# The forget gate's steps moved ahead of the first head pair's square, its memsets ahead of the mean square

## The chip, the cores and the metric

The kernel runs on one core of a Trainium2 chip. The metric is the device time of one execution in microseconds (us); what is quoted is the median of three runs. Everything is float32; to keep float32 accuracy on TensorE, most operands are split into a high and a low part, so that one product becomes three matmuls.

## The reference, cut to what matters

Two layers on a sequence of 1024 tokens with width 1024: first a short gated convolution, then an attention layer with a forget gate. The change touches the attention layer's start only.

```
h = rmsnorm(x, norm_g)
proj = h @ w_in                       # q | k | v | gate | forget, 4*1024 + 16 columns
q, k = rmsnorm(heads(q), q_g), rmsnorm(heads(k), k_g)     # per head of 64, 16 heads
log_f = log_sigmoid(proj[forget] + b_f)                   # 16 heads x 1024 tokens
c = cumsum(log_f, axis=tokens)
s = q @ k.T / 8 + c[query] - c[key]   # causal, then softmax, then @ v
x = x + (attention * silu(gate)) @ w_out
```

## The kernel before

All five engines have their instruction order written out by hand; they meet through counting semaphores (`s_f`, `s_fa` and so on), and each engine takes its instructions strictly in that order. Names used below: PE is TensorE, DVE VectorE, ACT ScalarE, POOL GpSimd, SP the engine that issues the loads and stores.

**Seam between the layers.** When the last convolution output has been added to `xy`, PE runs the 32 small matmuls of the forget columns (L686, into banks 4 and 5), then four of the mean square (L691). DVE meanwhile clears the stacks `q2`/`k2` with four memsets of 64 rows (`set_stacks(0.0, DH)`, L1604), adds EPS to the mean square (L1611), ACT makes a first guess of the reciprocal root as exp(-0.5 ln) (L1119, L1121), and DVE refines it to `inv`, the inverse norm of every token (L1614 to L1616). No projection can be evacuated before `inv` is there.

**Iteration 0 of the attention layer** projects the first head pair, and has no attention of its own. It has eight positions i = 0 to 7. At position i PE computes unit i, of 24 matmuls of 512 columns (L564): units 0 and 1 are the two halves of q, 2 and 3 of k, 4 and 5 of the gate, 6 and 7 of v. Units alternate between two banks, so unit i may start only when unit i - 2 has been evacuated by DVE (`qk_evac`, L1727; `vz_evac`, L1741). For each of the four q and k halves u the head norm follows, one position later each:

- ACT squares the half (`square`, L1295, at position u + 1), POOL makes the square's low part in two steps (`square_lo`, L1927, L1929),
- PE averages it over the head (`head_square`, L770 and L771), at position u + 2, between the fourth and the fifth eighth of that position's unit,
- ACT guesses the reciprocal root (`guess`, L1286, L1288), DVE refines it in four steps (`refine`, L1708 to L1714).

POOL's order is fixed too: `square_lo` of half 0 stands ahead of the low part of the weights for units 4 and 5 (`w_low`, L1907).

**The forget gate** is 16 rows of 1024 elements, and is worked out in iteration 0 in three parts, each of which DVE and ACT run at positions of their own. Part 0 on DVE (L1624 to L1633) adds the two halves of the logits, multiplies with `inv`, adds the bias, takes min(f, 0) and -|f|; part 0 on ACT is exp and ln(1 + .) (L1138, L1140). Part 1 on DVE fills `ones` with 1.0 (L1636), subtracts (L1638) and scans (L1640, the cumulative sum); on ACT it copies the high part of the sum (L1143). Part 2 is the low part (DVE, L1643) and the two negated copies (ACT, L1147, L1149). SP stores the four rows to `c_dram`, waits until all four have landed, and loads them into `q2` and `k2` (L469, L471). The first scores of iteration 1 (L714) wait for these rows. In DVE's position 1 stand four memsets of 4 rows that put 1.0 into `q2`/`k2` (`set_stacks(1.0, 4)`, L1604).

The positions of the parts are two short lists:

```
if not att and i in (2, 4, 5):        # DVE: parts 0, 1, 2
if not att and i in (3, 5, 6):        # ACT: parts 0, 1, 2
```

On ACT the part stands ahead of `square` of the same position. On DVE it stands behind the evacuation and `refine` of the same position. Iterations 1 to 8 run the attention of pair it - 1 beside the projection of pair it.

Of the kernel before, what the change touches and what calls it, by code (L numbers as in the profile page):

```python
# [7 lines left out]
ALU = mybir.AluOpType  # L8
ACT = mybir.ActivationFunctionType
# [5 lines left out]
KT = D // P  # L15
KH = KT // 2
NH = 16
# [90 lines left out]
def hybrid(nc, x, w_cin, w_cout, w_ain, w_forget, w_aout, conv_gain, conv_taps, attn_gain, b_forget,  # L108
# [5 lines left out]
    with ExitStack() as ctx:  # L114
        def sb(name, shape, dt=F32, where=ctx):
            return where.enter_context(nc.sbuf_tensor(name, shape, dt))

        def sem(name):
            return ctx.enter_context(nc.semaphore(name))
# [14 lines left out]
        b_f = sb("b_f", [NH, 1])  # L134
# [32 lines left out]
        y2 = sb("y2", [P, KT, S])  # L167
# [157 lines left out]
        def halves(h):  # L325
            return slice(h * HALF, (h + 1) * HALF)
# [49 lines left out]
        def _(sp):  # L376
# [77 lines left out]

            def store_c():

                sp.wait_ge(s_fa, 3)
                sp.dma_start(c_dram[:, 0, :], pt_hi[0:NH, :, :].bitcast(F32)).then_inc(s_cst, 16)
                sp.wait_ge(s_f, 8)
                sp.dma_start(c_dram[:, 1, :], pt_lo[0:NH, :, :].bitcast(F32)).then_inc(s_cst, 16)  # L460
                sp.wait_ge(s_fa, 4)
                sp.dma_start(c_dram[:, 2, :], v_st[0:NH, 0, :, :].bitcast(F32)).then_inc(s_cst, 16)
                sp.wait_ge(s_fa, 5)
                sp.dma_start(c_dram[:, 3, :], v_st[0:NH, 1, :, :].bitcast(F32)).then_inc(s_cst, 16)

            def c_rows(side, pair):
# [448 lines left out]
        def _(act):  # L915
            A = nc.scalar.activation
# [210 lines left out]
            def forget_low():  # L1127

                act.wait_ge(s_unit, 2 * N_FORGET + 2)
                for h in range(2):  # L1130
                    ins = A(p_big[0:NH, 1, halves(h)], ps[2 * NH:3 * NH, 4 + h, :], ACT.Copy)
                ins.then_inc(s_fc, 1)

            def forget(part):
                f = p_big[0:NH, 0, :]
                if part == 0:
                    act.wait_ge(s_f, 5)
                    A(f, f, ACT.Exp).then_inc(s_fa, 1)  # L1138
                    act.wait_ge(s_fa, 1)
                    A(f, f, ACT.Ln, bias=1.0).then_inc(s_fa, 1)  # L1140
                if part == 1:
                    act.wait_ge(s_f, 7)
                    A(pt_hi[0:NH, :, :], f.rearrange("p (a n) -> p a n", a=2), ACT.Copy).then_inc(s_fa, 1)  # L1143
                if part == 2:
                    act.wait_ge(s_fa, 3)
                    act.wait_ge(s_f, 8)
                    A(v_st[0:NH, 0, :, :], pt_hi[0:NH, :, :].bitcast(F32).rearrange("p a n -> p (a n)"),  # L1147
                      ACT.Copy, scale=-1.0).then_inc(s_fa, 1)
                    A(v_st[0:NH, 1, :, :], pt_lo[0:NH, :, :].bitcast(F32).rearrange("p a n -> p (a n)"),  # L1149
                      ACT.Copy, scale=-1.0).then_inc(s_fa, 1)  # L1150
# [70 lines left out]
            def iteration(it, proj, att, before):  # L1221
                for i in range(8):
# [29 lines left out]
                        guess(it, i - 2)  # L1252
                    if not att and i == 0:
                        forget_low()
                    if not att and i in (3, 5, 6):
                        forget((3, 5, 6).index(i))
                    if proj and i == (6 if att else 5):
                        stack_q_hi(it, 0)
                    if chunks > 2:
# [61 lines left out]
            with act.Fori(2, PAIRS) as it:  # L1321
                iteration(it, True, True, True)
# [11 lines left out]
        def _(dve):  # L1334
            v = nc.vector
            TT, TS, STT = v.tensor_tensor, v.tensor_scalar, v.scalar_tensor_tensor
# [262 lines left out]
            def set_stacks(value, rows):  # L1599

                for side in range(2):
                    r = DH * (1 - side)
                    for st in (q2, k2):
                        ins = v.memset(st[r:r + rows, side, :].bitcast(F32), value)  # L1604
                ins.then_inc(s_clear, 1)

            dve.wait_ge(s_co, 2 * KT)
            set_stacks(0.0, DH)
            for h in range(2):
                dve.wait_ge(s_ms, h + 1)  # L1610
                TS(mbuf[:, h, :], ps[:, 6 + h, :], EPS, None, ALU.add).then_inc(s_msr, 1)  # L1611
# [6 lines left out]
            def forget(part):  # L1618

                f, m0, ones = p_big[0:NH, 0, :], p_big[0:NH, 1, :], y2[0:NH, KT - 1, :]  # L1620
                if part == 0:
                    dve.wait_ge(s_fc, 1)
                    for h in range(2):
                        ins = TT(f[:, halves(h)], ps[0:NH, 4 + h, :], m0[:, halves(h)], ALU.add)  # L1624
                    ins.then_inc(s_f, 1)
                    dve.wait_ge(s_f, 1)
                    TT(f, f, inv[0:NH, :], ALU.mult).then_inc(s_f, 1)
                    dve.wait_ge(s_f, 2)
                    TS(f, f, b_f[:, :], None, ALU.add).then_inc(s_f, 1)
                    dve.wait_ge(s_f, 3)  # L1630
                    TS(m0, f, 0.0, None, ALU.min).then_inc(s_f, 1)
                    dve.wait_ge(s_f, 4)
                    STT(f, m0, 2.0, f, ALU.mult, ALU.subtract).then_inc(s_f, 1)  # L1633
                if part == 1:
                    dve.wait_ge(s_spill, 16 * KT)
                    v.memset(ones, 1.0)  # L1636
                    dve.wait_ge(s_fa, 2)
                    TT(m0, m0, f, ALU.subtract).then_inc(s_f, 1)  # L1638
                    dve.wait_ge(s_f, 6)
                    v.tensor_tensor_scan(f, ones, m0, 0.0, ALU.mult, ALU.add).then_inc(s_f, 1)  # L1640
                if part == 2:
                    dve.wait_ge(s_fa, 3)
                    TT(pt_lo[0:NH, :, :].rearrange("p a n -> p (a n)"), f,  # L1643
                       pt_hi[0:NH, :, :].bitcast(F32).rearrange("p a n -> p (a n)"), ALU.subtract)\
                        .then_inc(s_f, 1)
# [97 lines left out]
            def iteration(it, proj, att, before, base):  # L1743
                local = 0
                for i in range(8):
# [30 lines left out]
                        v_low(it - 1, 1)  # L1776
                    for c in range(2, chunks):
                        pt_low(own, at, c)
                    if not att and i == 1:
                        dve.wait_ge(s_clear, 1)  # L1780
                        set_stacks(1.0, 4)
                    if att:
                        invert(it, i, 1)
                    if proj and 2 <= i <= 5:
                        local = refine(it, i - 2, base, local)
                    if not att and i in (2, 4, 5):
                        forget((2, 4, 5).index(i))
                    if proj and i == 7:
                        stack_q_lo(it, 0)
                    if not proj and i == 0:  # L1790
# [235 lines left out]
```

## Time and profile before

| | |
|---|---|
| median of 3 runs | 1173.52 us (1173.18 to 1174.07) |
| the profiled execution | 1173.42 us, of which its span 1171.6 us |
| PE busy | 1130.5 us, 96% of the span |
| DVE, ACT, POOL busy | 775.2, 578.8, 608.1 us |
| iteration 0 on PE | about 438.4 to 491.45 us |
| mean granted TensorE clock | 0.991 |

The span runs from the first to the last instruction; the time of the execution is 1.8 us longer. A row of the timeline gives start, duration, engine, line, what is written and read, and in brackets how long the engine had been idle and who released it. Matmuls overlap, so a row of 0.39 us starts 0.23 us after the one before. In a row of the windows stand: the stretch, its length, busy time (and count) of PE, PE's weight loads, DVE, ACT and POOL, the granted TensorE clock (1.00 is 2.4 GHz), the DMA share and GB/s.

### The profile page before, as it was taken

To read this page: it belongs to the slowest core of one execution; us is meant where nothing else is said; L and a number is where in the kernel's file an instruction comes from. 1 tells how busy PE (TensorE), PEld (TensorE's weight loads), DVE (VectorE), ACT (ScalarE), POOL (GpSimd) and SP (SyncE) were. 2 spreads that over 40 slices of the span, in tenths; PEclk is the share of its full clock that TensorE was granted. 3 is DMA by queue.
4 is the path that set the end of the run, shared out by engine and by line. 5 is a ranking of instruction groups with operands and counts; after the bars stand their busy time and mean duration, and the time that the engine had idled before them with its cause. 6 is when DMAs were issued, how large, how long until landed. Compare 5 with 4: busy or idle time off the path is not lost.

```text
span 1171.6 us, 16915 instructions
## 1 busy us (share of the span) xinstructions
PE 1130.5 (96%) x5652; PEld 920.8 (79%) x5652; DVE 775.2 (66%) x1056; ACT 578.8 (49%) x982; POOL 608.1 (52%) x400
## 2 busy tenths in 40 slices
PE   5999999999999998999999999999999999978998
PEld 3688888888888876787887878878878788767887
DVE  3997778566865238668667586686675866875541
ACT  5553232333334324665755757657557575575410
POOL 2235665555546434556475664664755646655410
PEclk8999999999999999999999999999999999989999
DMA  6201102110144211200110101001101010002142
GB/s 216 73 1 72 70 4 72 72 72 19 54 162 151 92 58 63 58 26 19 38 37 1 42 31 37 18 18 36 36 2 52 19 36 18 18 18 89 56 160 75
DMA packets 20256, 64.17 MB, mean 55 GB/s; under 512 B 2928, under 2 KB 3056, under 8 KB 20208
## 3 DMA queue, kind: packets, MB, share of 16 engines
q1 hardware_dynamic: 20064, 63.53, 16.0%
q8 instruction: 29, 0.48, 0.2%
q14 instruction: 19, 0.16, 0.0%
q10 hardware_dynamic: 144, 0.00, 0.0%
HBM read 54.88 MB, written 8.65 MB: 54 GB/s over the span
## 4 chain that ended last, share of the span: by engine, by line
PE 85%; DVE 8%; issue 3%; ACT 2%; DMA 1%; POOL 1%; ACTq 0%; DVEq 0%; SPq 0%
PE ps L564 33%; PE ps L581 26%; PE ps L754 6%; PE ps L662 6%; PE ps L714 5%; PE ps L735 5%; DVE neg_max L1657 1%; DVE newton L1712 1%; PE ps L575 1%; PE ps L777 1%; PE ps L718 1%; PE ps L686 1%; DMA raw<-in_w_cout 1%; DVE b_lo L1502 1%; DVE newton L1708 1%
## 5 line engine op out<-in xcount | busy, mean ns | idle before, releaser
L564 PE MATMUL ps<-h_hi,w_hi 128*128 128x512 f32 x632 | 267.6, 423 | 5.8 <-DVE h_lo L1803 2.5
L564 PE MATMUL ps<-h_hi,w_lo 128*128 128x512 f32 x632 | 249.2, 394 | 0.0
L564 PE MATMUL ps<-h_lo,w_hi 128*128 128x512 f32 x632 | 248.4, 393 | 0.0
L1868 POOL TENSOR_TENSOR a_lo<-raw,a_hi 128x512 fp32r<-128x512 f32 x94 | 136.5, 1463 | 160.9 <-ACT a_hi L955 160.9
L581 PE MATMUL ps<-b_hi,a_hi 128*128 128x512 f32 x456 | 180.0, 395 | 8.0 <-DVE b_lo L1375 7.9
L581 PE MATMUL ps<-b_lo,a_hi 128*128 128x512 f32 x456 | 178.4, 391 | 0.0
L581 PE MATMUL ps<-b_hi,a_lo 128*128 128x512 f32 x456 | 178.3, 391 | 0.0
L564 PEld LDWEIGHTS ps<-h_hi,w_lo 128*128 128x128 f32 x632 | 119.1, 189 | 27.2
L1907 POOL TENSOR_TENSOR w_lo<-w_raw,w_hi 128x1024 fp32r<-128x1024 f32 x39 | 99.1, 2542 | 78.3 <-ACT w_hi L923 78.1
L1916 POOL TENSOR_TENSOR p_big<-p_big,rdenom 128x896 f32<-128x896 f32 (+1 forms) x64 | 93.8, 1466 | 87.8 <-DVE rdenom L1665 87.7
L1657 DVE TENSOR_REDUCE neg_max<-ps 128x1 f32<-128x896 f32 (+7 forms) x128 | 96.4, 753 | 62.3 <-PE ps L718 61.8
L564 PEld LDWEIGHTS ps<-h_hi,w_hi 128*128 128x128 f32 x632 | 120.2, 190 | 22.2 <-issue 3.6
L1671 DVE TENSOR_TENSOR pt_lo<-ps,pt_hi 128x512 fp32r<-128x512 f32 (+1 forms) x160 | 97.2, 633 | 53.4 <-ACT pt_hi L1180 51.1
L564 PEld LDWEIGHTS ps<-h_lo,w_hi 128*128 128x128 f32 x632 | 120.3, 190 | 15.0 <-issue 0.2
L1916 POOL TENSOR_TENSOR p_small<-p_small,rdenom 128x640 f32<-128x640 f32 (+1 forms) x64 | 70.6, 1104 | 115.6 <-DVE rdenom L1665 114.4
L955 ACT ACTIVATE a_hi<-raw 128x512 fp32r<-128x512 f32 x94 | 58.0, 628 | 121.5 <-PE ps L581 43.9
L581 PEld LDWEIGHTS ps<-b_hi,a_hi 128*128 128x128 f32 x456 | 86.1, 189 | 29.4 <-DVE b_lo L1375 10.3
L581 PEld LDWEIGHTS ps<-b_hi,a_lo 128*128 128x128 f32 x456 | 86.2, 189 | 18.2
L581 PEld LDWEIGHTS ps<-b_lo,a_hi 128*128 128x128 f32 x456 | 86.2, 189 | 17.9 <-issue 0.5
L1180 ACT ACTIVATE pt_hi<-ps 128x512 fp32r<-128x512 f32 (+1 forms) x160 | 83.1, 551 | 33.3 <-PE ps L735 31.9
L714 PE MATMUL ps<-k,q 128*128 128x512 f32 (+5 forms) x384 | 92.8, 351 | 5.8 <-ACT p_big L1170 3.6
L714 PEld LDWEIGHTS ps<-k,q 128*128 128x128 f32 x384 | 69.6, 191 | 23.4 <-ACT p_big L1170 7.0
(182 smaller groups left out, 2109.9 us busy)
## 6 DMA issues: line engine op xcount, KB each, us to landing
w_raw<-in_w_ain SPq DMA_DIRECT2D x32, 512.0 KB, 3.3
raw<-in_w_cin SPq DMA_DIRECT2D x28, 512.0 KB, 4.2
xy<-in_x SPq DMA_DIRECT2D x16, 512.0 KB, 4.7
raw<-in_w_cout SPq DMA_DIRECT2D x8, 512.0 KB, 4.4
x_dram<-xy SPq DMA_DIRECT2D x8, 512.0 KB, 4.2
w_raw<-in_w_aout SPq DMA_DIRECT2D x8, 512.0 KB, 4.3
out<-y SPq DMA_DIRECT2D x7, 512.0 KB, 7.1
raw<-in_w_cin SPq DMA_DIRECT2D x8, 256.0 KB, 8.6
```

Of the source, the lines that this page charges most:

```text
L564: last = mm(ps[:, bank, :], st[slot][:, k, :], mov(k)[:, halves(h)], start=(at == 0 and (when or k == 0) and st is w_hi and mov is mov_hi) ...
L581: ins = mm(ps[:, bank, :], st[:, i % RING, k, :], mov[:, k, :], start=(first and st is a_hi and mov is b_hi[b]), stop=(last and st is a_lo ...
L662: ins = mm(ps[:, BANKS[u % 8], :], st[:, i, k % KH, :], mov[Y_SLOT + s][:, 2 * c + h, :], start=(first and k == ks[0] and st is a_hi and m ...
L714: last = mm(ps[:, bank, 0:w], a[:, side, qs:qs + P], b[:, side, c * w:(c + 1) * w], start=(a is q1), stop=(a is q2 and not last_c))
L735: last = nc.tensor.transpose(ps[:, B_PT + g % 2, at:at + P], src[:, par, (2 * c + kp) * P:(2 * c + kp + 1) * P], ident[:, :])
L754: last = mm(ps[:, B_OUT, at + skip:at + 2 * P], v_st[:, side, 2 * c + kp, :], mov[:, g % 2, kp * 2 * P:(kp + 1) * 2 * P - skip], start=(c ...
L1180: A(pt_hi[:, g % 2, 0:w], ps[:, B_PT + g % 2, 0:w], ACT.Copy).then_inc(s_pth, 1)
L1657: v.tensor_reduce(neg_max[:, col:col + 1], src, ax, ALU.max, negate=True).then_inc(s_max, 1)
L1671: TT(pt_lo[:, g % 2, 0:w], ps[:, B_PT + g % 2, 0:w], pt_hi[:, g % 2, 0:w].bitcast(F32), ALU.subtract).then_inc(s_ptl, 1)
L1868: TT(a_lo[:, i % RING, :, :], entry_source(i), a_hi[:, i % RING, :, :].bitcast(F32), ALU.subtract).then_inc(s_alo, 1)
L1907: TT(w_lo[slot][:, :, :], w_raw[:, slot, :, :], w_hi[slot][:, :, :].bitcast(F32), ALU.subtract).then_inc(s_wlo, 1)
L1916: TT(p, p, rdenom[:, col:col + 1].broadcast_to([P, w]), ALU.mult).then_inc(s_pn, 1)
```

## The change

On DVE, the four memsets of 1.0 and the memset of `ones` move from positions 1 and 4 to a place behind the four of 0.0, ahead of the reading of the mean square. Part 0 of the forget gate moves from position 2 to 1 on DVE, parts 1 and 2 from 4 and 5 to 5 and 6. On ACT the parts move from 3, 5, 6 to 1, 6, 7. The bias addition and the minimum become one DVE instruction; the separate bias addition and the step to -|f| go, and ACT takes |f + b| itself, and gives exp a scale of -1. SP's waits are renumbered.

```
             def forget(part):                                        # ACT
                 f = p_big[0:NH, 0, :]
                 if part == 0:
-                    act.wait_ge(s_f, 5)
-                    A(f, f, ACT.Exp).then_inc(s_fa, 1)
+                    act.wait_ge(s_f, 3)
+                    A(f, f, ACT.Abs, bias=b_f[:, :]).then_inc(s_fa, 1)
                     act.wait_ge(s_fa, 1)
+                    A(f, f, ACT.Exp, scale=-1.0).then_inc(s_fa, 1)
+                    act.wait_ge(s_fa, 2)
                     A(f, f, ACT.Ln, bias=1.0).then_inc(s_fa, 1)
...
-                    if not att and i in (3, 5, 6):
-                        forget((3, 5, 6).index(i))
+                    if not att and i in (1, 6, 7):
+                        forget((1, 6, 7).index(i))
...
             dve.wait_ge(s_co, 2 * KT)
             set_stacks(0.0, DH)
+            dve.wait_ge(s_clear, 1)
+            set_stacks(1.0, 4)
+            v.memset(y2[0:NH, KT - 1, :], 1.0)
             for h in range(2):
                 dve.wait_ge(s_ms, h + 1)
                 TS(mbuf[:, h, :], ps[:, 6 + h, :], EPS, None, ALU.add).then_inc(s_msr, 1)
...
                     TT(f, f, inv[0:NH, :], ALU.mult).then_inc(s_f, 1)
                     dve.wait_ge(s_f, 2)
-                    TS(f, f, b_f[:, :], None, ALU.add).then_inc(s_f, 1)
-                    dve.wait_ge(s_f, 3)
-                    TS(m0, f, 0.0, None, ALU.min).then_inc(s_f, 1)
+                    TS(m0, f, b_f[:, :], 0.0, ALU.add, ALU.min).then_inc(s_f, 1)
+                if part == 1:
+                    dve.wait_ge(s_fa, 3)
+                    TT(m0, m0, f, ALU.subtract).then_inc(s_f, 1)
                     dve.wait_ge(s_f, 4)
-                    STT(f, m0, 2.0, f, ALU.mult, ALU.subtract).then_inc(s_f, 1)
-                if part == 1:
-                    dve.wait_ge(s_spill, 16 * KT)
-                    v.memset(ones, 1.0)
-                    dve.wait_ge(s_fa, 2)
-                    TT(m0, m0, f, ALU.subtract).then_inc(s_f, 1)
-                    dve.wait_ge(s_f, 6)
                     v.tensor_tensor_scan(f, ones, m0, 0.0, ALU.mult, ALU.add).then_inc(s_f, 1)
...
-                    if not att and i == 1:
-                        dve.wait_ge(s_clear, 1)
-                        set_stacks(1.0, 4)
...
-                    if not att and i in (2, 4, 5):
-                        forget((2, 4, 5).index(i))
+                    if not att and i in (1, 5, 6):
+                        forget((1, 5, 6).index(i))
```

DVE's instructions from the last memset of 0.0 to the first `refine`, before the change:

```order
L1604 MEMSET k2 64x1024
L1611 TENSOR_SCALAR sq2<-ps 128x512 [waits mean_square_done] x2
L1614 TENSOR_TENSOR acc<-inv 128x1024 [waits rsqrt_guessed]
L1615 SCALAR_TENSOR_TENSOR acc<-acc,sq2 128x1024 [waits vector_steps]
L1616 SCALAR_TENSOR_TENSOR inv<-acc,inv 128x1024 [waits vector_steps]
L1727 TENSOR_TENSOR qn<-ps,inv 128x512 [waits units_done,x1_stored,vector_steps]
L1604 MEMSET q2 4x1024 [waits stacks_cleared]
L1604 MEMSET k2 4x1024
...
L1727 TENSOR_TENSOR qn<-ps,inv 128x512 [waits units_done]
L1708 TENSOR_TENSOR newton<-y0 128x512 [waits head_rsqrt_guessed]
```

And after it (lines past the added ones are shifted by a few; L1726 is the evacuation, L1707 the first step of `refine`):

```order
L1606 MEMSET k2 64x1024
L1606 MEMSET q2 4x1024 [waits stacks_cleared]
L1606 MEMSET k2 4x1024
...
L1613 MEMSET y2 16x1024
L1616 TENSOR_SCALAR sq2<-ps 128x512 [waits mean_square_done] x2
L1619 TENSOR_TENSOR acc<-inv 128x1024 [waits rsqrt_guessed]
...
L1726 TENSOR_TENSOR qn<-ps,inv 128x512 [waits units_done,x1_stored,vector_steps]
L1629 TENSOR_TENSOR p_big<-ps,p_big 16x512 [waits forget_lo_part_copied]
...
L1632 TENSOR_TENSOR p_big<-p_big,inv 16x1024 [waits forget_steps]
L1634 TENSOR_SCALAR p_big<-p_big,b_f 16x1024 [waits forget_steps]
L1726 TENSOR_TENSOR qn<-ps,inv 128x512 [waits units_done]
L1707 TENSOR_TENSOR newton<-y0 128x512 [waits head_rsqrt_guessed]
```

Five memsets have come in front of the reading of the mean square, and four steps of the forget gate between the evacuations of units 0 and 1.

ACT's instructions from the guess for `inv` to the first head's guess, before:

```order
L1121 ACTIVATE inv<-inv 128x1024 [waits rsqrt_guessed]
L923 ACTIVATE w_hi0<-w_raw 128x1024 [waits units_done,w_landed0]
L1131 ACTIVATE p_big<-ps 16x512 [waits units_done]
...
L1295 ACTIVATE sq_hi<-qn 128x512 [waits qk_evacuated]
L923 ACTIVATE w_hi1<-w_raw 128x1024 [waits units_done,w_landed1]
L1286 ACTIVATE y0<-ps,eps_col 128x512 [waits head_square_done]
```

And after:

```order
L1121 ACTIVATE inv<-inv 128x1024 [waits rsqrt_guessed]
L923 ACTIVATE w_hi0<-w_raw 128x1024 [waits units_done,w_landed0]
L1131 ACTIVATE p_big<-ps 16x512 [waits units_done]
...
L1138 ACTIVATE p_big<-p_big,b_f 16x1024 [waits forget_steps]
L1140 ACTIVATE p_big<-p_big 16x1024 [waits forget_act_steps]
L1142 ACTIVATE p_big<-p_big 16x1024 [waits forget_act_steps]
L1297 ACTIVATE sq_hi<-qn 128x512 [waits qk_evacuated]
L923 ACTIVATE w_hi1<-w_raw 128x1024 [waits units_done,w_landed1]
L1288 ACTIVATE y0<-ps,eps_col 128x512 [waits head_square_done]
```

The three ACT steps of part 0 now stand in front of the square of the first q half; PE's and SP's orders are unchanged.

## Rows read from the trace of the kernel before

**Rows 1.** The page: busy time by engine, and the chain by engine.

```profile
PE 1130.5 (96%) x5652; PEld 920.8 (79%) x5652; DVE 775.2 (66%) x1056; ACT 578.8 (49%) x982; POOL 608.1 (52%) x400
...
PE 85%; DVE 8%; issue 3%; ACT 2%; DMA 1%; POOL 1%; ACTq 0%; DVEq 0%; SPq 0%
```

**Rows 2.** Timeline of PE in iteration 0: unit 2, head squares, waits, first scores.

```profile
449.70 0.39 PE L564 MATMUL ps<-h_hi,w_hi 128*128 128x512 f32 x1
...
452.42 0.39 PE L770 MATMUL ps<-sq_hi,mean_h 128*128 128x512 f32 x1
...
464.25 0.47 PE L564 MATMUL ps<-h_hi,w_hi 128*128 128x512 f32 x1 [2.42 <-DVE kn L1727]
...
469.32 0.47 PE L770 MATMUL ps<-sq_hi,mean_h 128*128 128x512 f32 x1 [2.09 <-POOL sq_lo L1929]
...
491.45 0.97 PE L714 MATMUL ps<-k,q 128*128 128x448 f32 x4
```

**Rows 3.** Windows: two stretches of iteration 0.

```profile
461.67:469.32 7.65, 3.14 (x13) 2.21 (x13) 5.73 (x8) 3.59 (x4) 2.97 (x3) 1.00 0.00 0
...
470.50:474.00 3.50, 3.50 (x10) 2.68 (x10) 2.46 (x4) 1.40 (x3) 2.94 (x3) 0.51 0.39 132
```

**Rows 4.** Timeline of DVE from the last memset of 0.0 to evacuation 1.

```profile
436.73 0.91 DVE L1604 MEMSET k<- 64x1024 f32 x1 [0.16 <-issue]
...
438.97 0.69 DVE L1611 TENSOR_SCALAR sq<-ps 128x512 f32<-128x512 f32 x1 [0.17 <-PE ps L691]
...
443.20 3.30 DVE L1615 SCALAR_TENSOR_TENSOR acc<-acc,sq 128x1024 f32<-128x1024 f32 x1
446.53 1.23 DVE L1616 SCALAR_TENSOR_TENSOR inv<-acc,inv 128x1024 f32<-128x1024 f32 x1
447.79 0.69 DVE L1727 TENSOR_TENSOR qn<-ps,inv 128x512 f32<-128x512 f32 x1
448.75 0.91 DVE L1604 MEMSET q<- 4x1024 f32 x1 [0.27 <-issue]
...
452.90 0.62 DVE L1727 TENSOR_TENSOR qn<-ps,inv 128x512 f32<-128x512 f32 x1
```

**Rows 5.** Timeline of DVE: the forget gate's parts 0 and 1.

```profile
458.24 1.27 DVE L1624 TENSOR_TENSOR p_big<-ps,p_big 16x512 f32<-16x512 f32 x2
459.54 1.21 DVE L1627 TENSOR_TENSOR p_big<-p_big,inv 16x1024 f32<-16x1024 f32 x1
460.79 0.74 DVE L1629 TENSOR_SCALAR p_big<-p_big,b_f 16x1024 f32<-16x1024 f32 x1
...
463.43 0.67 DVE L1727 TENSOR_TENSOR kn<-ps,inv 128x512 f32<-128x512 f32 x1
...
475.43 0.91 DVE L1636 MEMSET y<- 16x1024 f32 x1 [0.15 <-issue]
476.27 1.15 DVE L1638 TENSOR_TENSOR p_big<-p_big 16x1024 f32<-16x1024 f32 x1
477.46 2.28 DVE L1640 TENSOR_TENSOR_SCAN p_big<-y,p_big 16x1024 f32<-16x1024 f32 x1
```

**Rows 6.** Timeline of ACT: squares, part 0, the last copy.

```profile
448.52 0.63 ACT L1295 ACTIVATE sq_hi<-qn 128x512 fp32r<-128x512 f32 x1 [4.58 <-DVE qn L1727]
...
463.53 1.06 ACT L1138 ACTIVATE p_big<-p_big 16x1024 f32<-16x1024 f32 x1 [3.04 <-DVE p_big L1633]
...
465.58 0.61 ACT L1295 ACTIVATE sq_hi<-kn 128x512 fp32r<-128x512 f32 x1
...
485.34 1.04 ACT L1149 ACTIVATE v_st<-pt_lo 16x1024 fp32r<-16x1024 f32 x1
```

**Rows 7.** Timeline of POOL: the first low part of weights.

```profile
442.93 2.49 POOL L1907 TENSOR_TENSOR w_lo<-w_raw,w_hi 128x1024 fp32r<-128x1024 f32 x1 [10.33 <-ACT w_hi L923]
```

**Rows 8.** One line's instructions: L1714 on k (duration min/median/max in ns).

```profile
L1714 DVE SCALAR_TENSOR_TENSOR kn<-kn,gk,newton x16: 752/1082/1655, 473.6 to 1019.2; 128x512 f32<-128x512 f32 x16
```

**Rows 9.** Timeline of SP: the first load of the stored rows into k2.

```profile
488.64 0.24 SPq L471 DMA_DIRECT2D k<-c_dram  x1
```

More of the change, by code:

```diff
@@ L455, in store_c @@
             def store_c():
-                sp.wait_ge(s_fa, 3)
+                sp.wait_ge(s_fa, 4)
                 sp.dma_start(c_dram[:, 0, :], pt_hi[0:NH, :, :].bitcast(F32)).then_inc(s_cst, 16)
-                sp.wait_ge(s_f, 8)
+                sp.wait_ge(s_f, 6)
                 sp.dma_start(c_dram[:, 1, :], pt_lo[0:NH, :, :].bitcast(F32)).then_inc(s_cst, 16)
-                sp.wait_ge(s_fa, 4)
+                sp.wait_ge(s_fa, 5)
                 sp.dma_start(c_dram[:, 2, :], v_st[0:NH, 0, :, :].bitcast(F32)).then_inc(s_cst, 16)
-                sp.wait_ge(s_fa, 5)
+                sp.wait_ge(s_fa, 6)
                 sp.dma_start(c_dram[:, 3, :], v_st[0:NH, 1, :, :].bitcast(F32)).then_inc(s_cst, 16)
@@ L1136, in forget @@
                 if part == 0:
-                    act.wait_ge(s_f, 5)
-                    A(f, f, ACT.Exp).then_inc(s_fa, 1)
+                    act.wait_ge(s_f, 3)
+                    A(f, f, ACT.Abs, bias=b_f[:, :]).then_inc(s_fa, 1)
                     act.wait_ge(s_fa, 1)
+                    A(f, f, ACT.Exp, scale=-1.0).then_inc(s_fa, 1)
+                    act.wait_ge(s_fa, 2)
                     A(f, f, ACT.Ln, bias=1.0).then_inc(s_fa, 1)
                 if part == 1:
-                    act.wait_ge(s_f, 7)
+                    act.wait_ge(s_f, 5)
                     A(pt_hi[0:NH, :, :], f.rearrange("p (a n) -> p a n", a=2), ACT.Copy).then_inc(s_fa, 1)
                 if part == 2:
-                    act.wait_ge(s_fa, 3)
-                    act.wait_ge(s_f, 8)
+                    act.wait_ge(s_fa, 4)
+                    act.wait_ge(s_f, 6)
                     A(v_st[0:NH, 0, :, :], pt_hi[0:NH, :, :].bitcast(F32).rearrange("p a n -> p (a n)"),
@@ L1628, in forget @@
                     dve.wait_ge(s_f, 2)
-                    TS(f, f, b_f[:, :], None, ALU.add).then_inc(s_f, 1)
-                    dve.wait_ge(s_f, 3)
-                    TS(m0, f, 0.0, None, ALU.min).then_inc(s_f, 1)
+                    TS(m0, f, b_f[:, :], 0.0, ALU.add, ALU.min).then_inc(s_f, 1)
+                if part == 1:
+                    dve.wait_ge(s_fa, 3)
+                    TT(m0, m0, f, ALU.subtract).then_inc(s_f, 1)
                     dve.wait_ge(s_f, 4)
-                    STT(f, m0, 2.0, f, ALU.mult, ALU.subtract).then_inc(s_f, 1)
-                if part == 1:
-                    dve.wait_ge(s_spill, 16 * KT)
-                    v.memset(ones, 1.0)
-                    dve.wait_ge(s_fa, 2)
-                    TT(m0, m0, f, ALU.subtract).then_inc(s_f, 1)
-                    dve.wait_ge(s_f, 6)
                     v.tensor_tensor_scan(f, ones, m0, 0.0, ALU.mult, ALU.add).then_inc(s_f, 1)
                 if part == 2:
-                    dve.wait_ge(s_fa, 3)
+                    dve.wait_ge(s_fa, 4)
                     TT(pt_lo[0:NH, :, :].rearrange("p a n -> p (a n)"), f,
```

## The prediction, made before the changed kernel ran

> **What bounds the kernel now.** I read the page first: PE is busy for 96% of the span and holds 85% of the chain that ended last [rows 1]. So a change elsewhere counts only where PE waits for it, and the question is which waits PE has in iteration 0, the one place the change touches. The timeline of PE there shows two: 2.42 us for the evacuation of unit 2, which stood behind DVE's part 0 of the forget gate, and 2.09 us for POOL's low square, whose input stood behind ACT's exp and ln [rows 2]. The window over both has PE busy for 3.14 of 7.65 us, so 4.5 us are lost. Behind them the clock is granted at 0.51, which is the 1.2 GHz level, for the 3.5 us from 470.5; before this PE ran at full clock and had just been idle for most of 7.65 us [rows 3]. Half clock for 3.5 us loses about 1.7 us. Together some 6.2 us are to be had here, and the change removes all of these causes. What is left to ask is what it puts in their place.
>
> The reader should see next how thin the margin is one step earlier. Unit 2 starts at 449.70, and its bank is free since evacuation 0, which ran from 447.79 for 0.69 us: 1.2 us of slack. The head square stands 12 matmuls later, at 452.42, and PE takes it without a wait, 3.90 us after ACT began the square at 448.52 [rows 2, 4, 6]. POOL's two steps between them fill most of these 3.9 us (the same stretch takes 465.58 to 469.32, 3.74 us, where PE does wait [rows 2, 6]), so this margin is only some 0.2 us, and everything in front of it hangs on `inv`.
>
> **The change, part by part.**
>
> *The memsets.* DVE ran the last memset of 0.0 at 436.73 and read the second half of the mean square at 438.97, with under half a microsecond idle between: there is no idle stretch in front of the reading, it lies behind it. Four memsets of 4 rows took from 448.75 to 452.90, 4.15 us, and that of `ones` 0.84 us (475.43 to 476.27) [rows 4, 5]. Four rows cost as much as 64 (0.91 us either way). The new second reading starts at 436.73 + 1.04 + 4.15 + 0.84 + 0.62 (the first reading, like an evacuation) = 443.4, or up to 443.8 with the gaps that memsets leave between them; I take 443.6, 4.6 us late. `inv` follows at fixed steps, so evacuation 0 starts at 447.79 + 4.6 = 452.4. From an evacuation's start to PE's restart it is 464.25 - 463.43 = 0.82 us [rows 2, 5]: unit 2 starts at 453.2 instead of 449.70, **a new wait of 3.5 us**.
>
> One step of this chain can change its length. L1615 took 3.30 us while L1616, of the same size, took 1.23; from 442.93 to 445.42 POOL ran its weight step beside it [rows 4, 7]. Both engines are released by the same ACT steps, so both shift by 4.6 and meet again: I keep 3.30. The Trainium skill (SBUF — State Buffer, "Who interferes with whom") says that a DVE instruction with two SBUF inputs and a GpSimd one that reads SBUF hold each other off for a whole instruction, whichever starts first. By that rule, as by the row, the 3.30 stays; if the two no longer met, 2.1 us would come off and the result would be 1181.7.
>
> *Part 0 on DVE* now follows evacuation 0 at 452.4 + 0.69 = 453.1. Its steps: 1.30 for the two additions, 1.25 for the product, 0.74 for the fused bias and minimum (taken at the bias step's price) [rows 5]: done at 456.4. The two removed steps, 463.43 - (460.79 + 0.74) or 1.9 us, no longer count anywhere.
>
> *Part 0 on ACT.* Exp and ln took 465.58 - 463.53 = 2.05 us [rows 6]; |f + b| is a third step of that size, unseen so far, at 1.0. No table load stands in the order beside it. The square of half 0, which ACT used to begin at 448.52, now waits behind all three: 456.4 + 3.1 = 459.5, **11.0 us late**. Queued behind it are POOL's low square and POOL's weights for unit 4. With 3.74 us to the head square it runs at 463.25; PE, which reaches it at 453.2 + 2.72 = 455.9, **waits 7.3 us**. Altogether PE is then 463.25 - 452.42 = 10.8 us behind.
>
> *Iteration 0 from there.* Each position costs 26 matmuls of 0.227 us, 5.9 us (2.72 us for 12, rows 2), and the chain head square, guess, refine, next head square fits into that, as it did from 452.42 on. The removed steps no longer stand in the way, so the 4.5 us of old waits are gone. The fourth head square is at 463.25 + 17.7 = 480.95.
>
> *The end of the forget gate* now becomes late. From a head square to the end of refine: 469.32 to 475.43, 6.1 us with L1714 at its long 1.66, 5.2 at its short 0.75 [rows 2, 5, 8]; DVE alone at work, I take 5.2, giving 486.15. Part 1 adds 1.19 and 2.28 [rows 5]: 489.6. Then five ACT steps of 1.03 in a row, the high part, the two of stack k (which now stand in between), the two negated copies: 494.8. In the kernel before, ACT ended there at 485.34 + 1.04 = 486.38 and SP issued the load of the rows at 488.64 [rows 6, 9], 2.26 us later: 497.0. Its landing is not shown; it is at most 491.45 - 488.64 = 2.8 us, since the scores did not wait, and hardly under the 2.2 of the previous round trip, whose value I take: 499.2. PE has finished unit 7 at about 496, so it **waits 3 us more**, and the first scores come at 499.2 instead of 491.45 [rows 2]: 7.7 us late.
>
> *The clock.* Waits of 2.4 and 2.1 us were followed by 3.5 us at half clock [rows 3]. Now PE waits 3.5 and 7.3 us with 2.7 us of work between: a low stretch behind them is all but certain, 1.7 us; one inside that 2.7 us would be hidden by the wait that follows. Behind the last wait another low stretch is likely but not sure, up to 1.7; I take 1.0. Bounds are 0 and 3.4, perhaps 4.5 if the longer waits give longer stretches.
>
> *What is hidden.* Everything from iteration 1 on only shifts: PE is the chain there, and its waits in it are for engines that work from PE's own results. SP's weight load behind the stored rows shifts by the same amount as the scores.
>
> Sum: 7.7 + 1.7 + 1.0 = 10.4 us. Against the profiled execution, 1173.4, 1183.8; the median is 0.1 above that execution, so the number stands.
>
> **The rivals.**
>
> *The memsets cost nothing* (they start earlier, or run faster where nothing waits): then everything comes 4.6 us sooner, 1179.2. Against it: DVE had no 5 us free in front of 438.97.
>
> *ACT's square is not held by part 0*: if the forget logits were ready before `inv`, or ACT had the square done first, only the 3.5 us of unit 2 and the end of the forget gate would be left, some 5 or 6 us, 1179. Against it: the order puts three steps ahead, and L1627 needs `inv`. At 463.53 to 465.58 ACT ran exp and ln first though the k half was evacuated at 464.1 [rows 5, 6].
>
> *Not slower*: what is added in front of the first head square is small. This decides at about 2.8 us: from a head square at 455.2 instead of 463.25 the same chain of steps reaches the scores at 491.2, and with nothing added, up to the margin, at about 488.5, which is 3 us faster, 1170.5. For it speaks that 6.2 us of losses do vanish; against it, that the five memsets alone are 5 us and three ACT steps 3.1.
>
> *More lost than this*: if |f| brings a table load or is slow, or a longer low clock follows each wait, 1187 to 1188.
>
> **How the numbers follow.** Forecast 0.78, with its own range of 1180.5 to 1186.5 (no low stretch and a short landing to longer ones); memsets free 0.07; square not held 0.06; not slower 0.05; worse 0.04. The range 1179.0 to 1186.5 holds the forecast and most of the two milder cases. 0.2% is 2.35 us, about what a measurement of this kernel can tell. Not slower splits into 0.02 faster and 0.03 same; all else is slower, 0.95.
>
> **What the profile would show.** The second reading of the mean square near 443.6; unit 2 at about 453.2, released by evacuation 0; the first `head_square` near 463.3 with PE idle for 7 us in front of it, released by POOL, after a square near 459.5; no waits at units 4 and head squares 2; PEclk near 0.5 behind it; scores near 500 to 502, released by the load of the stored rows. The prediction is wrong if the reading still comes near 439, or if the head square starts before 456.

## The result and the profile after

The changed kernel takes 1184.78 us (median of 6 runs, 1183.79 to 1185.80) against 1173.91 us for the kernel before (6 runs): 10.9 us more, ratio 1.0094 with a 95% interval of 1.0084 to 1.0104. (This ratio and those below come from all runs of both kernels; they differ by up to 0.0005 from the quotient of the two medians.) The forecast was 1183.8, or 10.4 us more.

In the profiled executions the first scores begin at 502.82 us instead of 491.45 [rows 2], 11.4 us later, and the span grows by 11.4 us as well, from 1171.6 to 1183.0. So in these two executions all of the loss arises before the first scores of iteration 1, and nothing is won or lost behind them.

PE's waits in iteration 0 of the changed kernel, from the view of who waited for whom in the stretch from 437 to 505 us (total, times, longest):

```profile
PE ps L770 <- POOL sq_lo L1925: 4.9, 1, 4.9
PE ps L564 <- DVE qn L1726: 3.5, 1, 3.5
PE ps L564 <- DVE y L1740: 2.4, 1, 2.4
PE ps L714 <- DMA k<-c_dram: 1.1, 1, 1.1
```

Both old waits [rows 2] are gone, and four new ones of 11.9 us in total stand in their place, in the order of the list: at the first head square, at unit 2, at unit 7, and at the first scores.

The timeline of DVE shows the first of them arise; the five memsets fill the time up to the reading of the mean square [rows 4]:

```profile
436.82 0.91 DVE L1606 MEMSET k<- 64x1024 f32 x1 [0.16 <-issue]
438.00 0.91 DVE L1606 MEMSET q<- 4x1024 f32 x1 [0.27 <-DVE k L1606]
...
442.38 0.91 DVE L1613 MEMSET y<- 16x1024 f32 x1 [0.16 <-issue]
443.22 1.21 DVE L1616 TENSOR_SCALAR sq<-ps 128x512 f32<-128x512 f32 x2
...
451.30 1.23 DVE L1621 SCALAR_TENSOR_TENSOR inv<-acc,inv 128x1024 f32<-128x1024 f32 x1
452.56 0.69 DVE L1726 TENSOR_TENSOR qn<-ps,inv 128x512 f32<-128x512 f32 x1
...
455.72 0.74 DVE L1634 TENSOR_SCALAR p_big<-p_big,b_f 16x1024 f32<-16x1024 f32 x1
```

Evacuation 0 starts at 452.56 instead of 447.79. Then part 0 on DVE ends at 456.46, and the timeline of ACT has the three steps ahead of the square:

```profile
456.50 1.15 ACT L1138 ACTIVATE p_big<-p_big,b_f 16x1024 f32<-16x1024 f32 x1 [7.78 <-DVE p_big L1634]
...
459.73 0.61 ACT L1297 ACTIVATE sq_hi<-qn 128x512 fp32r<-128x512 f32 x1
```

ACT had been idle for 7.78 us. The square comes 11.2 us later than at 448.52 [rows 6]. PE's timeline:

```profile
453.40 0.47 PE L564 MATMUL ps<-h_hi,w_hi 128*128 128x512 f32 x1 [3.46 <-DVE qn L1726]
...
462.85 0.80 PE L770 MATMUL ps<-sq_hi,mean_h 128*128 128x512 f32 x1 [4.86 <-POOL sq_lo L1925]
...
494.35 0.50 PE L564 MATMUL ps<-h_hi,w_hi 128*128 128x512 f32 x1 [2.36 <-DVE y L1740]
...
502.82 1.04 PE L714 MATMUL ps<-k,q 128*128 128x448 f32 x4 [1.11 <-DMA k<-c_dram]
```

The window over three stretches gives the clock (columns as before: busy time and count of each engine, then the granted clock):

```profile
453.40:457.59 4.19, 4.19 (x12) 3.28 (x12) 3.59 (x5) 1.09 (x1) 0.00 (x0) 0.59 0.00 0
...
464.00:468.00 4.00, 4.00 (x12) 3.14 (x11) 2.41 (x4) 1.84 (x3) 2.99 (x3) 0.55 0.42 131
495.00:498.40 3.40, 3.40 (x10) 2.65 (x9) 2.87 (x3) 3.36 (x4) 1.43 (x1) 0.51 0.24 39
```

PE ran a stretch at half clock behind each of its three waits of more than 2 us. The first is hidden: PE reaches the first head square later, and waits 4.9 us there instead of the 7.3 forecast, but the head square itself is on time. The second counts in full: the granted clock is 0.51 from 462.85 to 467.66, and the next head square comes 8.2 us behind the first (471.08) where it came 5.95 us behind in the kernel before, so 2.3 us are lost. The third lies inside unit 7 and shortens the wait for the stored rows.

The end of the gate holds the one surprise, in the timelines of DVE and POOL:

```profile
489.34 4.37 DVE L1639 TENSOR_TENSOR_SCAN p_big<-y,p_big 16x1024 f32<-16x1024 f32 x1
```

```profile
488.14 3.43 POOL L1903 TENSOR_TENSOR w_lo<-w_raw,w_hi 128x1024 fp32r<-128x1024 f32 x1 [5.64 <-ACT w_hi L923]
```

The scan took 4.37 us instead of 2.28 [rows 5], because POOL's step on the weights now runs beside it. In the kernel before it could not: ACT's part 1, which waits for the scan, stood ahead of the high part of the weights (L923), and POOL waits for that. The timelines of ACT and POOL before:

```profile
479.77 1.06 ACT L1143 ACTIVATE pt_hi<-p_big 16x1024 fp32r<-16x1024 f32 x1 [0.82 <-DVE p_big L1640]
...
482.64 1.04 ACT L923 ACTIVATE w_hi<-w_raw 128x1024 fp32r<-128x1024 f32 x1
```

```profile
483.76 2.80 POOL L1907 TENSOR_TENSOR w_lo<-w_raw,w_hi 128x1024 fp32r<-128x1024 f32 x1 [9.03 <-ACT w_hi L923]
```

In the changed kernel ACT's part 1 stands one position later, behind L923, and ACT makes the high part of the weights before the scan begins:

```profile
487.02 1.04 ACT L923 ACTIVATE w_hi<-w_raw 128x1024 fp32r<-128x1024 f32 x1
```

The other runs agree: the scan took 4.35 to 4.38 us in the three further versions below whose ACT part 1 is in position 6 and whose POOL is not held, and 2.28 us in all those where it is in position 5.

### The profile page after: what moved, and what is told of

The parts are those of the page before. It is cut to its first block, busy times and chain, and to the rows that moved or that the text cites. A ratio compares the mean times of both kernels' runs of the same rounds, so it can differ in the third digit from the quotient of the medians.

```text
span 1183.0 us, 16914 instructions
## 1 busy us (share of the span) xinstructions
PE 1135.3 (96%) x5652; PEld 923.8 (78%) x5652; DVE 776.0 (66%) x1054; ACT 579.7 (49%) x983; POOL 609.7 (52%) x400
## 4 chain that ended last, share of the span: by engine, by line
PE 83%; DVE 9%; issue 3%; ACT 2%; DMA 1%; POOL 1%; ACTq 0%; SPq 0%; DVEq 0%
PE ps L564 32%; PE ps L581 25%; PE ps L754 6%; PE ps L662 6%; PE ps L714 5%; PE ps L735 5%; DVE neg_max L1656 1%; DVE newton L1711 1%; PE ps L575 1%; PE ps L777 1%; PE ps L718 1%; DVE b_lo L1504 1%; DMA raw<-in_w_cout 1%; PE ps L770 1%; PE ps L771 1%
## 5 line engine op out<-in xcount | busy, mean ns | idle before, releaser
L581 PEld LDWEIGHTS ps<-b_hi,a_hi 128*128 128x128 f32 x456 | 86.1, 189 | 29.2 <-DVE b_lo L1377 10.3
```

Source lines behind the costliest of these rows:

```text
L581: ins = mm(ps[:, bank, :], st[:, i % RING, k, :], mov[:, k, :], start=(first and st is a_hi and mov is b_hi[b]), stop=(last and st is a_lo ...
```

## The experiments

The theory: the loss is the sum of two delays in front of the first head square, the memsets ahead of the mean square and the gate's part 0 ahead of the head norms, less the two old waits, plus a late end of the gate. Its rivals: one of the two is hidden; the arithmetic (a slow absolute value) is what costs; only the place of one ACT instruction matters. Each ratio below is to the kernel before on the same chip. Starts in different profiles can be off by 1 to 2 us as a whole, since the convolution's start differs, so waits and distances are compared.

**mem_early**: the kernel before, with only the memsets moved.

```
             set_stacks(0.0, DH)
+            dve.wait_ge(s_clear, 1)
+            set_stacks(1.0, 4)
+            v.memset(y2[0:NH, KT - 1, :], 1.0)
...
-                    v.memset(ones, 1.0)
...
-                    if not att and i == 1:
-                        dve.wait_ge(s_clear, 1)
-                        set_stacks(1.0, 4)
```

> The kernel before with one part of the change alone: the five memsets (four of 1.0, one of ones) ahead of the reading of the mean square. Theory (DVE has no idle stretch there, so inv comes 4.8 us later and everything with it): second reading at 443.8, a new PE wait of 3.5 us at unit 2, the two old waits (units 4 and head square 2) still there; first scores 4.5 us later than before, time +4.5 us (+3.5 to +6.5 with low-clock stretches). Rival (the memsets fit beside other work; the whole loss is the forget gate's part 0): +0 to +1 us, inv at 447.8 as before.

Measured: 1179.40 against 1174.29, +5.1 us, ratio 1.0048 (1.0031 to 1.0065). PE's timeline:

```profile
452.00 0.52 PE L564 MATMUL ps<-h_hi,w_hi 128*128 128x512 f32 x1 [3.45 <-DVE qn L1728]
...
468.25 0.47 PE L564 MATMUL ps<-h_hi,w_hi 128*128 128x512 f32 x1 [2.38 <-DVE kn L1728]
...
473.33 0.47 PE L770 MATMUL ps<-sq_hi,mean_h 128*128 128x512 f32 x1 [0.57 <-POOL sq_lo L1927]
```

The wait at unit 2 is there, the old ones too. The second is shorter, since PE came to it at half clock: here that low stretch is hidden in the wait, and the profiled execution was the fastest of the four, 1176.18 against 1179.39 to 1179.65. The rival that the memsets are hidden is out.

**gate_only**: the changed kernel with the memsets back in iteration 0.

```
-            dve.wait_ge(s_clear, 1)
-            set_stacks(1.0, 4)
-            v.memset(y2[0:NH, KT - 1, :], 1.0)
...
+                    v.memset(ones, 1.0)
                     dve.wait_ge(s_fa, 3)
...
                     if not att and i in (1, 5, 6):
                         forget((1, 5, 6).index(i))
+                    if not att and i == 1:
+                        dve.wait_ge(s_clear, 1)
+                        set_stacks(1.0, 4)
```

> The changed kernel with the memsets back inside iteration 0 (the four behind part 0 in position 1, that of ones in part 1), so that the gate's new places and its new ACT step act alone. Theory (ACT's square of half 0 waits for part 0, whatever inv does): inv at 447.8 again, no wait at unit 2, the square at 455, the first head square at 458.2 with a PE wait of about 5.7 us, first scores 7.3 us later than before, time +7.3 us (+6 to +8.5). Rival (the memsets alone make the loss; the gate's steps fit in): time within 1.5 us of before.

Measured: 1179.80 against 1174.29, +5.5 us, ratio 1.0049 (1.0032 to 1.0066); under the forecast of +7.3 and under its range of +6 to +8.5, though far from the rival. The structure is as expected: ACT's three steps stand ahead of the square, the first head square waits 5.50 us for POOL:

```profile
458.86 0.80 PE L770 MATMUL ps<-sq_hi,mean_h 128*128 128x512 f32 x1 [5.50 <-POOL sq_lo L1926]
```

The profiled execution was the slowest of the four, 1182.34 and so +8, with 13 matmuls at half clock behind this wait and a second wait of 3.4 us at unit 7, where the scan again took 4.35 us; the others took 1179.1 to 1180.0. Why they were 2.4 us or more faster is not shown, since only one was profiled. With mem_early the two parts add up to 10.6 us, and the change costs 10.9; the intervals of the two are some 2 us wide each way, so this sum is no proof that nothing else is in it.

**square_first**: the changed kernel with ACT's part 0 behind the square of position 1.

```
-                    if not att and i in (1, 6, 7):
+                    if not att and i in (6, 7):
                         forget((1, 6, 7).index(i))
...
                     if proj and 1 <= i <= 4:
                         square(it, i - 1)
+                    if not att and i == 1:
+                        forget(0)
```

> The changed kernel with ACT's part 0 behind the square of half 0 in position 1 instead of ahead of it; nothing else changed. Theory (the hold-up is ACT's strict order, but DVE's refine and the square of half 1 then wait behind the same three steps): first head square at about 456.5 instead of 462.9 with almost no wait, but a wait of about 2.5 us at the second one; the end of the gate (scan, copies, stored rows) as late as before relative to the fourth head square; time 2.7 us under the changed kernel, +8.6 over the kernel before. Rival (the position of the square is the whole of it): 6 us or more under the changed kernel.

Measured: 1184.60 against 1174.29, +10.3 us, ratio 1.0087 (1.0070 to 1.0104). The theory had +8.6, the rival +5 or less: neither came true, nothing was won. ACT's and PE's timelines:

```profile
454.03 0.63 ACT L1299 ACTIVATE sq_hi<-qn 128x512 fp32r<-128x512 f32 x1 [4.57 <-DVE qn L1728]
458.58 1.15 ACT L1138 ACTIVATE p_big<-p_big,b_f 16x1024 f32<-16x1024 f32 x1 [3.92 <-DVE p_big L1636]
...
462.89 0.69 ACT L1290 ACTIVATE y<-ps,eps_col 128x512 f32<-128x512 f32 x1
```

```profile
458.35 0.60 PE L770 MATMUL ps<-sq_hi,mean_h 128*128 128x512 f32 x1
...
469.04 0.80 PE L770 MATMUL ps<-sq_hi,mean_h 128*128 128x512 f32 x1 [4.37 <-DVE qn L1715]
...
502.24 1.06 PE L714 MATMUL ps<-k,q 128*128 128x448 f32 x4 [2.64 <-DMA k<-c_dram]
```

The first head square no longer waits, but its guess (L1290) now stands behind the gate's steps, and the second head square waits 4.37 us for the refine that follows. In this order the block was only passed on to the next in line. Two steps of DVE's part 0 also met POOL here (1.64 and 1.66 us instead of 1.21 and 0.74), and so did refine's first (1.60 instead of 0.69).

**act_late**: ACT's part 0 behind the last square instead, the memsets still early.

```
-                    if not att and i in (1, 6, 7):
+                    if not att and i in (6, 7):
                         forget((1, 6, 7).index(i))
...
                     if proj and 1 <= i <= 4:
                         square(it, i - 1)
+                    if not att and i == 4:
+                        forget(0)
```

> The changed kernel with one thing moved: ACT's part 0 of the gate stands behind the square of position 4, so behind all four squares; DVE's part 0 stays in position 1, and the five memsets stay early. Theory (after the memsets the loss is ACT's part 0 in front of the head norms): wait of 3.5 us at unit 2 stays, no wait over 1 us at any head square, the wait at unit 7 of about 2.5 us and a short one for the stored rows stay; first scores 4.3 us later than in the kernel before, time +4.3 (+3.3 to +6) against it, about 7 us under the changed kernel. Rival (DVE's part 0 in position 1 is what holds up the chain, since the version with the square ahead of ACT's part gave nothing): a head square still waits 4 us or more, time within 3 us of the changed kernel.

Measured: 1177.60 against 1173.47, +4.1 us, ratio 1.0034 (1.0022 to 1.0047). No head square waits:

```profile
452.60 0.52 PE L564 MATMUL ps<-h_hi,w_hi 128*128 128x512 f32 x1 [3.46 <-DVE qn L1728]
457.02 0.39 PE L770 MATMUL ps<-sq_hi,mean_h 128*128 128x512 f32 x1
...
463.02 0.50 PE L770 MATMUL ps<-sq_hi,mean_h 128*128 128x512 f32 x1
```

The forecast was +4.3, and it holds: with ACT's block behind the squares, some 6.8 us of the change's 10.9 are gone (each to the kernel before of its own runs), and DVE's part 0 in position 1 costs nothing that can be seen. What is left is the memsets' 3.46 us at unit 2 and the end of the gate, with waits of 2.33 us at unit 7 and 1.02 us for the stored rows, less the old waits. The later places of parts 1 and 2 were not run by themselves, so their share is read from these waits alone.

**fused_in_place**: the change's arithmetic at the old places (positions 2, 4, 5 on DVE, 3, 5, 6 on ACT, memsets as before).

```
-                    if not att and i in (1, 5, 6):
-                        forget((1, 5, 6).index(i))
+                    if not att and i in (2, 4, 5):
+                        forget((2, 4, 5).index(i))
...
-                    if not att and i in (1, 6, 7):
-                        forget((1, 6, 7).index(i))
+                    if not att and i in (3, 5, 6):
+                        forget((3, 5, 6).index(i))
```

> The change's arithmetic alone: bias and minimum in one DVE instruction, the absolute value on ACT, but parts and memsets at the places of the kernel before. Theory: DVE's part 0 is 1.9 us shorter, so the wait at unit 4 falls from 2.4 to about 0.7 us, but ACT's part 0 is one step longer, so the square of half 2 is hardly sooner and its head square waits about 3.2 us; time -0.8 us against before (-2 to +0.5). Rival (the arithmetic is what costs in the changed kernel, such as a slow absolute value): +1 us or more.

Measured: 1171.98 against 1172.92, -0.9 us, ratio 0.9990 (0.9980 to 0.9999). The wait at unit 4 is 0.46 us instead of 2.42, that of head square 2 is 2.78 instead of 2.09, and unit 6 now waits 1.67 us. The waits come to 4.9 us against 4.5 in the kernel before, so the profiled gain is not from shorter waits; what this execution lacks is the low stretch of [rows 3], its clock stays at 1.00 from 462.5 to 490.4. The absolute value is not the cost; it took 1.15 us.

**scan_alone**: the changed kernel, POOL's step held until the scan is done.

```
+                    if not att and i == 6:
+                        pool.wait_ge(s_f, 5)
                     if proj and i % 2 == 0:
                         w_low(
```

> The changed kernel with one more wait: POOL's low part of the weights in position 6 waits for the scan, so that the two do not run side by side. The scan took 4.37 us in the changed kernel beside POOL's step of 3.43, and 2.28 in the kernel before with POOL idle. Theory (the two hold each other off): the scan takes 2.3 us, the wait at unit 7 shrinks from 2.4 to about 0.4 us, first scores and time about 2 us sooner than the changed kernel, +9.3 over before. Rival (the scan is long for another reason, such as its place): scan still 4.4 us, time unchanged against the changed kernel or slightly worse.

Measured: 1184.87 against 1174.29, +10.6 us, ratio 1.0093 (1.0076 to 1.0110): the same as the changed kernel. Yet the scan is short again:

```profile
488.85 2.28 DVE L1639 TENSOR_TENSOR_SCAN p_big<-y,p_big 16x1024 f32<-16x1024 f32 x1
...
491.76 0.50 PE L564 MATMUL ps<-h_hi,w_hi 128*128 128x512 f32 x1 [0.27 <-DVE y L1740]
...
500.68 1.37 PE L714 MATMUL ps<-k,q 128*128 128x448 f32 x4 [3.18 <-DMA k<-c_dram]
```

So the meeting of DVE and POOL makes the scan long, as the theory had it; the forecast of time (2 us sooner, +9.3) failed. The 2.1 us went in two ways. POOL's step now met DVE's part 2, which took 2.42 us instead of 1.22, and some 0.4 us of this reached the first scores: from the first head square to the first scores it is 38.3 us instead of 40.0, 1.7 sooner and not 2.1. And the wait moved from unit 7 to the stored rows, where it is 3.18 us long, and behind it the clock is low. The window of 5.4 us from the first scores, here and in the changed kernel:

```profile
500.60:506.00 5.40, 5.32 (x17) 3.93 (x17) 1.85 (x3) 2.01 (x3) 3.65 (x2) 0.68 0.43 142
```

```profile
502.80:508.20 5.40, 5.38 (x29) 4.08 (x29) 2.01 (x4) 2.65 (x5) 4.08 (x2) 1.00 0.47 147
```

(1.00 - 0.68) x 5.4 = 1.7 us are lost there, all that was left of the scan's gain. In the changed kernel the low stretch had fallen into unit 7, where the wait for the rows hid it.

**best1, best2, best2_side**: versions that follow the theory. In best1, ACT's part 0 stands behind the square of position 4, part 1 at the end of position 5 and part 2 in position 6; DVE's part 0 in position 1, part 1 ahead of refine in position 5, part 2 ahead of the evacuation in position 6; two memsets stand behind the reading of the mean square, two behind part 0. best2 sets the memsets one by one, moves DVE's part 2 and adds a wait on POOL (best2_side is best2 without that wait):

```
             dve.wait_ge(s_clear, 1)
+            v.memset(q2[DH:DH + 4, 0, :].bitcast(F32), 1.0)
+            v.memset(k2[DH:DH + 4, 0, :].bitcast(F32), 1.0)
             dve.wait_ge(s_rs0, 2)
...
+                    if not att and i == 1:
+                        forget(0)
+                        v.memset(y2[0:NH, KT - 1, :], 1.0)
+                    if not att and i == 3:
+                        v.memset(q2[0:4, 1, :].bitcast(F32), 1.0)
+                    if not att and i == 4:
+                        v.memset(k2[0:4, 1, :].bitcast(F32), 1.0).then_inc(s_clear, 1)
+                    if not att and i == 5:
+                        forget(1)
                     if proj and 2 <= i <= 5:
                         local = refine(it, i - 2, base, local)
+                    if not att and i == 5:
+                        forget(2)
...
+                    if not att and i == 6:
+                        pool.wait_ge(s_f, 6)
                     if proj and i % 2 == 0:
                         w_low(
```

> A version that follows the theory: two of the memsets in the stretch where DVE waits for ACT's guess of inv, two behind DVE's part 0; DVE's part 0 in position 1 behind the evacuation; ACT's part 0 behind the square in position 4, its part 1 behind stack q in position 5, part 2 in position 6; DVE's part 1 ahead of refine in position 5 and part 2 ahead of the evacuation in position 6. Theory: inv at about 447.8 to 448, no wait at units 2, 4 and no head square late, a wait of about 1 us at unit 7, no low clock; first scores 5 us sooner than in the kernel before, time -5 us (-3 to -6). Rival (something else bounds iteration 0, such as the port shared by DVE and POOL or the end of the gate): within 1.5 us of before.

> The first improved version with its three remaining waits taken on: the memsets one by one in stretches where DVE waits (two behind the reading of the mean square, the one of ones behind part 0, one each in positions 3 and 4); DVE's parts 1 and 2 on both sides of refine in position 5; POOL's low part of the weights in position 6 waits until DVE's part 2 is done, so that the two do not meet. Theory: the low part of the sum takes 1.2 us instead of 3.4, no PE wait over 1 us in iteration 0, no low clock; first scores at about 485.7 to 486.5, 5 us sooner than before, time -5 us (-3.5 to -6.5). Rival (the end of iteration 0 is bound by the stored rows or by what iteration 1 needs from POOL, whose step is now later): -1 to -2.5 us like the first improved version.

> The same version without POOL's added wait, so that POOL's weight step runs beside DVE's part 2. Theory (the two hold each other off, and part 2 stands ahead of the evacuation that frees unit 7's bank): part 2's low copy takes 3 us or more instead of 1.2, unit 7 waits about 1.5 to 2 us and the stored rows come 2 us later; time 1.5 to 3 us over the version with the wait. Rival (no contention): the same time as the version with the wait.

best1 measured 1171.82 against 1172.92, -1.1 us, ratio 0.9986 (0.9977 to 0.9996). The forecast of -5 (-3 to -6) failed, and the rival, which named the port shared by DVE and POOL or the end of the gate, came true. The head norms are clean (one wait of 1.01 us), but DVE's part 2, placed ahead of the evacuation that unit 7 needs, met POOL's weight step: 3.39 us instead of 1.21, and unit 7 waited 2.86 us with a low clock behind it. One wait of 1 us at unit 7 and no low clock had been expected.

best2 measured 1168.57 against 1173.47, **-4.9 us, ratio 0.9956 (0.9943 to 0.9969)**, where -5 was forecast; best2_side 1170.04, -3.4 us, ratio 0.9967 (0.9955 to 0.9980), 1.5 us slower than best2 on the same chip, at the lower end of the 1.5 to 3 forecast. Their runs overlap (1166.76 to 1169.66 and 1168.92 to 1171.47), so the size of this difference is less sure than its cause, which the rows show. DVE's part 2 in best2, then in best2_side:

```profile
477.02 1.21 DVE L1644 TENSOR_TENSOR pt_lo<-p_big,pt_hi 16x1024 fp32r<-16x1024 f32 x1
```

```profile
477.39 3.42 DVE L1644 TENSOR_TENSOR pt_lo<-p_big,pt_hi 16x1024 fp32r<-16x1024 f32 x1
```

All of PE's waits of best2 from 437 to 486 us, and the window over it:

```profile
PE ps L714 <- POOL k L1942: 0.5, 1, 0.5
PE ps L770 <- DVE qn L1715: 0.3, 1, 0.3
```

```profile
437.00:491.00 54.00, 53.20 (x234) 41.81 (x233) 43.76 (x45) 31.93 (x38) 28.18 (x15) 1.00 0.21 66
```

The clock stays at 1.00. In best2_side unit 7 waits 1.91 us for the evacuation behind the long part 2.

## Why the prediction was right, step by step

**The memsets.** Forecast: reading of the second half at 443.6, unit 2 at 453.2 with a 3.5 us wait. The profile has 443.8, 453.40 and 3.46. mem_early shows the part alone, +5.1 us.

**Part 0 ahead of the square.** Forecast: the square at 459.5 and the head square at 463.25. The profile has 459.73 and 462.85. The step in between was priced from a passage of 3.74 us; here it took 3.12, with POOL's first step at 1.04 us, which had taken 1.56 beside refine in the passage that was used. The margin at the first head square in the kernel before was therefore 3.90 - 3.12 = 0.8 us, not the 0.2 that the prediction read. gate_only (+5.5) and act_late (+4.1, with this block taken away) show the cause.

**The old waits go.** Right: no wait at unit 4 or at head squares 1 to 3.

**The rule of the shared port.** L1620, the second refining step of `inv`, met POOL again and took 3.30 us again (a row of the chain gives 3.31 us at 447.97), as row and rule both had it. But the prediction applied the rule at the one place where the trace before showed a collision, and not at the steps that were moved. The Trainium skill (SBUF — State Buffer, "Who interferes with whom") says it of every DVE instruction with two SBUF inputs beside a GpSimd one that reads SBUF. The traces agree for the scan (4.37 us) and for part 2 (3.39 and 3.42 us), which both read two operands from SBUF.

**The end of the gate: a term mis-sized.** "Part 1 adds 1.19 and 2.28 ... 489.6" was 1.24 and 4.37, 2.1 us more, and the landing taken at 2.2 us was 1.7 (501.11 to 502.82). The 2.2 called that of the previous round trip was not one: from the last store's issue at 486.41 to the first load's at 488.30 it is 1.9 us. POOL's passage made the first head square 0.4 us sooner, and refine took 0.2 us less. The way through the head squares was 0.9 us longer than 17.7 + 1.7 (483.11 - 462.85 = 20.3), most of it since the low stretch cost 2.3 us and not 1.7. The late scan also held up unit 7 by 2.36 us, where the prediction had no wait and scan_alone has 0.27.

**The clock.** Two stretches that count, 1.7 and 1.0, were forecast. One counts, the one behind the head square, at 2.3 us; the last wait is only 1.1 us and the clock behind it is full.

**What was luck.** The mechanism of the two big delays was right and shown. That the sum came so close is in part luck: the scan (+2.1) and the head squares (+0.9) were put too low, the last low stretch (1.0), the landing (0.5), POOL's passage (0.4) and refine (0.2) too high, and these errors of some 3 and 2 us nearly cancel. In the changed kernel's profile 7.7 + 1.7 + 1.0 = 10.4 became 11.4, in the medians 10.9.

**The rivals.** "The memsets cost nothing" is out by mem_early. "ACT's square is not held" is out, since the square came at 459.73. Its price of 1179 holds only if nothing else of the norms is held either: act_late, with the block behind all squares, is at +4.1 us, but with only the first square put ahead the time stays at 1184.6. What the rival left out is the guess that stands behind the same block. "Not slower" is out for this kernel. The 6.2 us of old losses that spoke for it can be had in another order: best2, with nothing ahead of the norms, is 4.9 us faster, somewhat more than the 3 us that the prediction gave the case with nothing added.

## What to carry to other kernels

- A stretch is idle for an instruction only where the engine waits behind it in the order too: look at what reads its engine next, not at the idle share of a slice. Here the 2.3 us of waiting lay one instruction later, and five memsets of 1 us stood in front of the one chain that everything hung on.
- Before a block moves on an in-order engine, list the steps that will now stand behind it, and for each when another engine needs it; moving the block past one instruction can merely hand the delay on, as in square_first. List also what the move lets go earlier: here ACT's part 1 had kept POOL's weight step away from the scan.
- A saved wait is worth its length only if the next step is not held in turn and what follows runs at full clock: in scan_alone a gain of 2.1 us in one step gave nothing in the time.

## What the runs showed of the hardware that had not been expected

- DVE instructions with two SBUF operands took 2.1 to 2.2 us more when they met the beginning of a POOL step over 128x1024: the scan 4.37 instead of 2.28, the low copy of 16x1024 3.39 and 3.42 instead of 1.21. Holding POOL back brought the scan to 2.28 (scan_alone) and the low copy to 1.21 (best2). Sixteen rows are held up as long as 128 (L1620, 3.30 instead of 1.23). The rows show how the length comes about: POOL's step ended at 491.57 and the scan at 493.71, 2.14 us later, about its own length; L1620 ended 1.08 us after POOL's step (450.19 and 451.27). So what is added is what was left of POOL's step. It also goes the other way: POOL's step that began 0.04 us after L1637 took 3.43 us, against 2.4 in best2. In square_first L1636, with one tensor operand and the bias column, took 1.66 us beside POOL instead of 0.74, so more than steps with two tensor operands are held; this was not run by itself.
- Waits of PE of 1.9 us (best2_side) and 2.8 us (fused_in_place) left the clock at full level in the profile, while waits of 2.4 us in the changed kernel and 2.3 us in act_late were followed by seven matmuls at half clock. The same wait at unit 7 can go either way: in square_first it was 2.34 us and the clock behind it 1.00. The length of one wait alone did not tell in these traces whether the clock would fall.
- Executions of one kernel differ by more than the smaller effects here: the kernel before ran from 1171.62 to 1176.41 us on one chip. This goes with the clock: its 14 runs up to 1173.08 us had a mean granted clock of 0.991 to 0.993, its 7 runs from 1174.93 us one of 0.987 to 0.989. Another part arises ahead of the change: unit 0 starts at 437.06 us in mem_early's profile and at 439.19 in square_first's, behind the same instructions, with a granted clock of 0.93 and of 0.90 in the first 50 us.
